# Norming the tokens of the last three experts apart, and finishing every other row while those experts still run

## The chip, the cores and the metric

The kernel runs on one core of a Trainium2 chip. The metric is the device time of one execution in microseconds (us). Before the change it is 1068.41 us, the median of 3 runs (1067.77 to 1070.65). TensorE is called PE, VectorE DVE, ScalarE ACT, GpSimd POOL, and SyncE SP. A DMA is issued by SP or, when its rows are picked by a list of indices, by POOL ("indirect").

## The reference

One layer of a hybrid decoder is computed for 1024 prompt tokens and 64 sample tokens of width 1024, all in float32: a mixing stage, cross-attention, and then the stage that matters here, a mixture of 32 experts in 4 groups, followed by the final norm.

```python
def hier_moe(x, w_rg, b_rg, w_re, b_re, w_e1, w_e3, w_e2):
    ...                                   # top-1 of 4 groups, top-2 of 8 experts within it
    for g in range(N_GROUPS):
        a = jnp.einsum('nd,edf->nef', xf, w_e1[g])
        b = jnp.einsum('nd,edf->nef', xf, w_e3[g])
        hid = jax.nn.silu(a) * b * gates[:, g, :, None]
        y = y + jnp.einsum('nef,efd->nd', hid, w_e2[g])
...
    x = x + hier_moe(rmsnorm(x, g_ffn), w_rg, b_rg, w_re, b_re, w_e1, w_e3, w_e2)
...
    y_prompt = rmsnorm(xp, g_final)       # x * rsqrt(mean(x*x) + 1e-6) * g_final, row by row
    y_sample = rmsnorm(xs, g_final)
```

A token gets rows from exactly two experts, both of one group.

## The kernel before, in words

Everything up to the routing fills the first 713 us. Then the loop over the experts runs (`e` from 0 to 31). Experts are taken in turn from the four groups (`expert_at`), so the last three (`e` = 29, 30, 31) belong to three different groups, and a token's other expert always lies a multiple of four steps away. An expert works on up to 128 listed tokens. Its steps are:

- POOL gathers the normed rows of its tokens from DRAM (`rows_in`, helper line 2466).
- PE turns them, and multiplies them with the "up" weights (`ab`); ACT applies SiLU (`sil`, line 1542), DVE multiplies the halves (`hid`, line 2314), PE turns the result (`hidden`, line 918), and ACT and DVE split it into a high and a low part (`hidden_left`, line 1206, and `hidden_lo`, line 2303).
- PE multiplies with the "down" weights one expert later (`yy(e - 1)`, matmuls in lines 525 to 527). Each product is made of three matmuls, because values are split into high and low parts; ACT (`part_to_hi`, line 1525) and DVE (`up_lo`, `down_lo`, lines 2292 and 2298) split every weight chunk of 128 x 1024.
- ACT scales the two halves of the result, 128 x 512 each, by the gates (`y_left`, line 1548), and POOL adds the rows to a DRAM tensor `token_sums` with an indirect DMA that accumulates (`rows_out`, line 2471). `token_sums` held x before the loop.

All engines run their own instruction streams in program order and meet by semaphores: `m_sc[0]` and `m_sc[1]` count landed scatters of even and odd experts, `m_w[s]` the weight loads, `m_used` the weight chunks that PE is done with, `m_yo0` and `m_yo1` the drained halves of the result. A weight chunk lies in one of 28 slots of a ring (`part_raw`).

After the loop, POOL waits until all 32 scatters have landed, and then lets the others go (`o_go`). A block for tokens that didn't fit into 128 slots ("spill") is skipped here. SP then loads the nine tiles of `token_sums` (8 of 128 prompt rows, one of 64 sample rows; line 989), ACT squares and sums each tile (line 1611) and takes roots for groups of tiles (`NORMS`, line 1614), DVE makes inverse roots in five small instructions (lines 2382 and 1632 to 1635) and scales each tile (line 2386), and SP stores it (line 1199).

Of the kernel before, what the change touches and what calls it, by code (L numbers as in the profile page):

```python
# [33 lines left out]
ALU = mybir.AluOpType  # L34
# [24 lines left out]
LG = 40  # L59
NEG = -3.0e38  # L60
# [22 lines left out]
def trunk_step(nc, i_, o_):  # L83
    ctx = ExitStack()
    with ctx:
# [210 lines left out]
        junk = regS[:, 4 * D:5 * D]  # L296
        gfin = regA[:, 7168:8192]
        NORMS = [(0, 2), (2, 3), (5, 3), (8, 1)]
# [68 lines left out]
        s_cst, s_pv, s_xh = sem("s_cst"), sem("s_pv"), sem("s_xh")  # L367
# [88 lines left out]
        s_moe = sem("s_moe")  # L456
# [18 lines left out]
        def sums_back(eng, t):  # L475

            eng.wait_ge(m_w[t], 16 * (len(range(t, 3 * NE, RAW // 2)) + 1))
# [12 lines left out]
        def _(pe):  # L490
# [435 lines left out]
            def yy(e):  # L926

                s = e % 2
                pe.wait_ge(m_hl, e + 1)
                if e >= 1:  # L930
                    pe.wait_ge(m_yo0, e)
                    pe.wait_ge(m_yo1, e)
                for c in range(2):
                    n = part_no["down", e, c]
                    hi, lo = part_hi[n % HI], part_lo[n % RAW]
                    pe.wait_ge(m_dl, 2 * e + c + 1)
                    for h in range(2):
                        product(bank[B_Y[h]][:, :], (HThi[s][:, c, :], HTlo[s][:, c, :]),
                                (hi[:, 512 * h:512 * h + 512], lo[:, 512 * h:512 * h + 512]),
                                c == 0, c == 1, m_used if h else None)  # L940
# [29 lines left out]
            pe.wait_ge(o_go, 1)  # L970
            n_spill = pe.value_load(spx[0:1, 16:17], min_val=0, max_val=SPILL)
            with pe.If(n_spill > 0):
                with pe.Fori(0, SPILL) as q:
# [13 lines left out]
        def _(sp):  # L987
# [23 lines left out]
            load(Y_f[:, 0:4, cols_of(0)], i_["xt"][:, 0:4, cols_of(0)], s_xh)  # L1011
# [168 lines left out]
            n_spill = sp.value_load(spx[0:1, 16:17], min_val=0, max_val=SPILL)  # L1180
            with sp.If(n_spill > 0):
                with sp.Fori(0, SPILL) as q:
# [9 lines left out]
            sp.wait_ge(s_moe, 1)  # L1192
            for t in range(NT):
                load(X[0:rows_of(t), t], sum_dram[P * t:P * t + rows_of(t), :], m_w[t])
            for t in range(NT):
                sp.wait_ge(s_fo, t + 1)
                dst = o_["y_prompt"][0, P * t:P * t + P, :] if t < NPT else \
                    o_["y_sample"].rearrange("b s d -> (b s) d")
                sp.dma_start(dst, X[0:rows_of(t), t]).then_inc(s_fst, 16)
            sp.wait_ge(s_fst, 16 * NT)  # L1200
# [3 lines left out]
        def _(act):  # L1204
# [45 lines left out]
            for h, landed in ((0, s_xh), (1, s_x[0])):  # L1250
# [315 lines left out]
            for e in range(2):  # L1566
                act.wait_ge(m_tx, e + 1)
                for q in range(2):
                    token_hi(e, q)
                if e == 0:  # L1570
                    part_to_hi("down", 0, 0)
                    part_to_hi("down", 0, 1)
            for e in range(NE):
                used(act, ("up", e, 3))
                sil(e % 2, B_AB[e % 2], m_sil)
                if e + 2 < NE:
                    part_to_hi("up", e + 2, 0)
                    act.wait_ge(m_tx, e + 3)
                    token_hi(e + 2, 0)
                    token_hi(e + 2, 1)  # L1580
                    part_to_hi("up", e + 2, 1)
                if e >= 1:
                    y_left(e - 1)
                if e + 2 < NE:
                    part_to_hi("up", e + 2, 2)
                hidden_left(e)
                if e + 2 < NE:
                    part_to_hi("up", e + 2, 3)
                if e + 1 < NE:
                    part_to_hi("down", e + 1, 0)  # L1590
                    part_to_hi("down", e + 1, 1)
            y_left(NE - 1)
            act.wait_ge(o_go, 1)
            n_spill = act.value_load(spx[0:1, 16:17], min_val=0, max_val=SPILL)
            with act.If(n_spill > 0):
                with act.Fori(0, SPILL) as q:
# [7 lines left out]
            nc.scalar.activation(small[:, 2:3], small[:, 0:1], ACT.Sqrt)  # L1604
            for t0, n in NORMS:
                for t in range(t0, t0 + n):
                    r = rows_of(t)
                    sums_back(act, t)
                    if t > 0:
                        act.wait_ge(s_fsq, t)  # L1610
                    nc.scalar.activation(junk[0:r, :], X[0:r, t, :], ACT.Square,  # L1611
                                         accum_out=stat[0:r, t:t + 1]).then_inc(s_fsq, 1)
                act.wait_ge(s_fsq, t0 + n)
                nc.scalar.activation(stat[0:r, 10 + t0:10 + t0 + n], stat[0:r, t0:t0 + n], ACT.Sqrt,  # L1614
                                     scale=1.0 / D, bias=small[0:r, 0:1]).then_inc(s_frt, 1)
# [3 lines left out]
        def _(dve):  # L1619
# [715 lines left out]
            down_lo(0, 1)  # L2335
            for e in range(NE):
                dve.wait_ge(m_sil, e + 1)
                hid(e % 2, B_AB[e % 2], m_hid)
                if e + 2 < NE:
# [3 lines left out]
                    up_lo(e + 2, 1)  # L2343
                hidden_lo(e)
# [3 lines left out]
                if e + 1 < NE:  # L2348
                    down_lo(e + 1, 0)
                    down_lo(e + 1, 1)  # L2350
                if e in (5, 8, 11):
                    place_in_table((e - 5) // 3)
                if e == 16:
                    spill_counts()
# [10 lines left out]
            dve.wait_ge(o_go, 1)  # L2365
            n_spill = dve.value_load(spx[0:1, 16:17], min_val=0, max_val=SPILL)
            with dve.If(n_spill > 0):
                with dve.Fori(0, SPILL) as q:
# [6 lines left out]


            def finish(g):
                t0, n = NORMS[g]
                r = rows_of(t0)
                dve.wait_ge(s_frt, g + 1)  # L2380
                a, root, r0, tmp, out = (stat[0:r, c + t0:c + t0 + n] for c in (280, 10, 300, 310, 20))
                link(ts_(a, stat[0:r, t0:t0 + n], 1.0 / D, EPS, ALU.mult, ALU.add))  # L2382
                inv_root(a, root, r0, tmp, out)
                for j in range(n):
                    x = X[0:r, t0 + j, :]
                    stt(x, x, out[:, j:j + 1], gfin[0:r, :], ALU.mult, ALU.mult).then_inc(s_fo, 1)  # L2386

            dve.wait_ge(s_cst, 32)
            for g in range(len(NORMS)):
                finish(g)  # L2390
# [3 lines left out]
        def _(g):  # L2394
# [5 lines left out]
            g.memset(bst[:, :], 1.0)  # L2400
            g.memset(lgm[:, :], 0.0)
# [42 lines left out]
            g.sem_inc(o_y, 1)  # L2444
# [10 lines left out]
            last_token, last_gate = g.to_reg(N - 1), g.to_reg(2 * P * NT - 1)  # L2455
            g.wait_ge(s_xnd[0], 16 * 5)
# [34 lines left out]

            rows_in(0)
# [6 lines left out]
            for e in range(NE):  # L2499
                if e + 4 < NE:  # L2500
                    rows_in(e + 4)
                if e >= 1:
# [11 lines left out]
            g.sem_inc(o_go, 1)  # L2514
# [12 lines left out]
            g.sem_inc(s_moe, 1)  # L2527
# [100 lines left out]
```

## Time and profile before

| | |
|---|---|
| median of 3 runs | 1068.41 us |
| the profiled execution | 1065.81 us |
| its span, first to last instruction | 1064.0 us |
| PE busy | 999.0 us (94%), 5327 matmuls |
| DVE busy | 638.3 us (60%) |
| ACT busy | 541.6 us (51%) |
| POOL busy | 197.6 us (19%) |
| last matmul starts | 1031.31 us |
| last store is issued | 1060.74 us |

The span is what the trace covers; the 1.8 us between it and the execution's own time are outside of it. A row of the timeline gives start, duration, engine, line, operation and what is written from what; in brackets stands how long the engine had been idle and what released it. Adjacent instructions of an engine overlap a little, so a series of the same kind is shorter than the sum of its durations.

### The profile page before, as it was taken

How to read it: one execution, taken by the hardware profiler on the slowest of the kernel's cores; microseconds unless marked ns; L12 is line 12 of the kernel's file. 1: busy time of each engine (PE TensorE's matmuls, PEld its weight loads, DVE VectorE, ACT ScalarE, POOL GpSimd, SP SyncE). 2: the span in 40 equal slices, each digit the busy share in tenths (PEclk: the TensorE clock that was granted, in tenths of full speed). 3: DMA queues.
4: the chain of work that ended last, by engine and by line, in shares of the span. 5: the costliest groups of instructions: out<-in, count | busy, mean ns of one | idle time of the engine just before them, and what ended most of it. 6: DMA issues, size and time to landing. Idle time of an engine off the chain costs nothing. (4 is left out here: it accounts for less than half of the span.)

```text
span 1064.0 us, 14237 instructions
## 1 busy us (share of the span) xinstructions
PE 999.0 (94%) x5327; PEld 848.1 (80%) x5327; DVE 638.3 (60%) x1175; ACT 541.6 (51%) x918; POOL 197.6 (19%) x136
## 2 busy tenths in 40 slices
PE   8999999999999999999999999948999999999970
PEld 6998999798887689999655878847888888888850
DVE  4526756345654650002664125677999999999935
ACT  6644333305221532213545012255999999999944
POOL 0003211100000021200000300011333375642220
PEclk9999999999999999999999999967999999999995
DMA  9701111244000653103563005487999999999738
GB/s 314 217 1 59 57 42 40 99 139 173 1 1 0 225 177 113 40 20 127 232 256 139 1 37 201 159 310 300 396 392 391 384 364 390 382 387 393 284 55 335
DMA packets 55211, 203.06 MB, mean 191 GB/s; under 512 B 10710, under 2 KB 19423, under 8 KB 41575
## 3 DMA queue, kind: packets, MB, share of 16 engines
q1 hardware_dynamic: 44327, 181.61, 44.9%
q0 software_dynamic: 10816, 20.54, 7.6%
q8 instruction: 43, 0.70, 0.3%
q14 instruction: 25, 0.20, 0.1%
HBM read 185.06 MB, written 32.83 MB: 205 GB/s over the span
## 5 line engine op out<-in xcount | busy, mean ns | idle before, releaser
L527 PE MATMUL bank<-regA_r,regW_r 128*128 128x352 f32 (+1 forms) x456 | 148.8, 326 | 0.0
L526 PE MATMUL bank<-regA_r,regW_r 128*128 128x352 f32 (+1 forms) x456 | 148.7, 326 | 0.0
L359 POOL TENSOR_TENSOR regW_r<-regW,regW_r 128x1024 fp32r<-128x1024 f32 x19 | 47.1, 2477 | 348.7 <-ACT regW_r L346 348.6
L1525 ACT ACTIVATE regY_r<-expert_w 128x1024 fp32r<-128x1024 f32 x105 | 108.9, 1062 | 1.0 <-PE bank L527 0.9
L525 PE MATMUL bank<-expert_w_r,regS_r 128*128 128x512 f32 x256 | 103.4, 404 | 0.0
L1525 ACT ACTIVATE regW_r<-expert_w 128x1024 fp32r<-128x1024 f32 x87 | 90.2, 1061 | 6.7 <-PE bank L527 6.7
L2292 DVE TENSOR_TENSOR expert_w_r<-expert_w,regY_r 128x1024 fp32r<-128x1024 f32 x74 | 89.0, 1218 | 0.0
L525 PE MATMUL bank<-regY_r,regW_r 128*128 128x352 f32 (+1 forms) x264 | 87.3, 331 | 0.5 <-ACT regB L1206 0.5
L526 PEld LDWEIGHTS bank<-regA_r,regW_r 128*128 128x128 f32 x456 | 85.9, 188 | 0.4
L527 PEld LDWEIGHTS bank<-regA_r,regW_r 128*128 128x128 f32 x456 | 85.6, 188 | 0.0
L2466 POOL DMA_INDIRECT regW<-normed_tokens,idx x32 | 44.0, 1374 | 200.0 <-DVE idx L2201 119.6
L1215 ACT ACTIVATE regS<-regX 128x1024 f32<-128x1024 f32 (+1 forms) x17 | 18.0, 1060 | 119.9 <-DVE regX L1877 119.9
L527 PE MATMUL bank<-regW_r,regA_r 128*128 128x384 f32 (+3 forms) x216 | 76.4, 354 | 0.0
L2471 POOL DMA_INDIRECT token_sums<-regS,idx x32 | 55.5, 1735 | 106.2 <-ACT regS L1548 102.6
L1877 DVE TENSOR_TENSOR regX<-regX,bank 128x512 f32<-128x512 f32 (+1 forms) x36 | 24.1, 686 | 77.8 <-PE bank L527 77.7
L527 PE MATMUL bank<-regY_r,regS_r 128*128 128x512 f32 x180 | 70.4, 391 | 0.0
L526 PE MATMUL bank<-regY_r,regB_r 128*128 128x512 f32 (+1 forms) x176 | 68.6, 390 | 0.0
L1952 DVE TENSOR_REDUCE stat<-bank 128x2 f32<-128x512 f32 x16 | 11.0, 690 | 93.9 <-PE bank L699 93.9
L2292 DVE TENSOR_TENSOR expert_w_r<-expert_w,regW_r 128x1024 fp32r<-128x1024 f32 x54 | 64.8, 1217 | 0.0
L527 PE MATMUL bank<-regY_r,regA_r 128*128 128x512 f32 (+1 forms) x164 | 64.0, 390 | 0.0
L525 PE MATMUL bank<-regB_r,regW_r 128*128 128x352 f32 (+1 forms) x192 | 63.0, 328 | 0.0
L526 PE MATMUL bank<-regY_r,regS_r 128*128 128x512 f32 x148 | 57.7, 390 | 0.0
(363 smaller groups left out, 2408.1 us busy)
## 6 DMA issues: line engine op xcount, KB each, us to landing
expert_w<-in_we SPq DMA_DIRECT2D x96, 1024.0 KB, 13.3
regY<-in_cache_mem_v SPq DMA_DIRECT2D x6, 1024.0 KB, 7.2
regW<-in_wbc SPq DMA_DIRECT2D x11, 512.0 KB, 3.6
regS<-in_x_prompt SPq DMA_DIRECT2D x8, 512.0 KB, 6.5
regX<-in_x_prompt SPq DMA_DIRECT2D x8, 512.0 KB, 6.6
regW<-in_wq SPq DMA_DIRECT2D x8, 512.0 KB, 3.6
regA<-in_kct SPq DMA_DIRECT2D x4, 1024.0 KB, 7.9
token_sums<-regX SPq DMA_DIRECT2D x8, 512.0 KB, 2.9
```

The costliest lines, as they stand in the source:

```text
L359: eng.tensor_tensor(lo, raw, hi.bitcast(F32), ALU.subtract).then_inc(w_lo[name], 1)
L525: nc.tensor.matmul(out, stays[0], moves[1], start=first, stop=False)
L526: nc.tensor.matmul(out, stays[1], moves[0], start=False, stop=False)
L527: ins = nc.tensor.matmul(out, stays[0], moves[0], start=False, stop=last)
L1215: nc.scalar.activation(dst[0:r, :], src[0:r], ACT.Square, accum_out=stat[0:r, c:c + 1]).then_inc(s_sq[s], 1)
L1525: nc.scalar.activation(part_hi[u % HI], part_raw[n % RAW], ACT.Copy).then_inc(m_wh, 1)
L1877: tt(x, x, ps[0:r, :], ALU.add).then_inc(sg, 1)
L1952: link(nc.vector.tensor_reduce(stat[:, 276:278], ps[:, :].rearrange("p (a m) -> p a m", a=2), axis=AX.X, op=ALU.max, negate=True))
L2292: tt(part_lo[n % RAW], part_raw[n % RAW], part_hi[u % HI].bitcast(F32), ALU.subtract).then_inc(m_ul, 1)
L2466: g.indirect_dma_start(out=XG[s], out_offset=None, in_=xn_dram, in_offset=bass.IndirectOffsetOnAxis(ap=ix[:, 0:1], axis=0), bounds_check=l ...
L2471: g.indirect_dma_start(out=sum_dram, out_offset=bass.IndirectOffsetOnAxis(ap=ix[:, 0:1], axis=0), in_=YO[s], in_offset=None, bounds_check= ...
```

## The change

The tokens of the last three experts (`LATE = 3`) are kept out of `token_sums`. Their sums so far are gathered into SBUF early, DVE adds the last expert rows to them there, and these three blocks of 128 rows are normed and written by indirect DMAs straight to the outputs. The nine tiles are loaded as soon as the scatters of experts 0 to 28 have landed, are normed, and are stored as before; the rows in them that belong to late tokens are stale and are overwritten afterwards. Dead slots of the weight ring hold all of it (`spot`).

- POOL: at `e` = 28, after `rows_out(27)`, `late_sums()` gathers three times; `rows_out` of 29, 30 and 31 are gone. At the end, `samples_out(0)`, `samples_out(1)`, a wait for all prompt stores (`s_fst`), `prompt_out(0)` to `(2)`, `samples_out(2)`: six indirect DMAs. The wait for all of them stands ahead of the spill block.
- SP: loads of `gfin` and the nine tiles move ahead of the end of the loop; stores follow in the order of `UNITS` (sample tile, prompt tiles 0 to 7).
- ACT: `y_left` of 29, 30 and 31 is gone. Three squares stand at the end of `e` = 30, ahead of `sil(31)`. Behind `sil(31)` come the table load for Sqrt, the first root and a fourth square, ahead of `hidden_left(31)`. Eight more squares and three roots follow the loop.
- DVE: `rows_left(29)`, `(30)`, `(31)` add `bank * gate` to the gathered rows. Units 0 and 1 are multiplied by `gfin` ahead of time (`weighted`), so that a plain scaling is left. Four groups of inverse roots (`ROOTS`) and twelve scaled blocks instead of nine. Two small index operations come at `e` = 14 (`late_samples`).
- PE: the first half of the last expert's result is signalled by itself. The spill block is taken only if there is a spill, on every engine.

```diff
@@ names
+LATE = 3
-        NORMS = [(0, 2), (2, 3), (5, 3), (8, 1)]
+        LAST = len(PARTS) - RAW
+        def spot(j):
+            return part_raw[(LAST + j) % RAW]
+        UNITS = [("tile", t) for t in (NPT, *range(NPT))] + [("rows", k) for k in range(LATE)]
+        ROOTS = [(0, 3), (3, 4), (7, 1 + LATE), (NT + LATE - 1, 1)]
+        AHEAD, WEIGHTED = (3, 2) if LATE > 2 else (0, 0)
@@ sync
-            used(sp, ("down", NE - 1, 1))
+            for n in range(NT):
+                weights_landed(sp, n)
+            spot_dead(sp, GFIN_AT)
             load(gfin, i_["gfin"], s_cst)
-            sp.wait_ge(o_go, 1)
+            for q in range(2):
+                sp.wait_ge(m_sc[q], 16 * len(range(q, NE - LATE, 2)))
...
+            for u, (_, t) in enumerate(UNITS[:NT]):
+                spot_dead(sp, XF_AT + u)
+                sums_load(t)
+            for u, (_, t) in enumerate(UNITS[:NT]):
+                sp.wait_ge(s_fo, u + 1)
+                final_store(t)
@@ scalar, in the loop over e
+                if e == NE - 1:
+                    nc.scalar.activation(small[:, 2:3], small[:, 0:1], ACT.Sqrt)
+                    if AHEAD:
+                        roots(*ROOTS[0])
+                        square(AHEAD)
-                if e >= 1:
+                if 1 <= e <= NE - LATE:
                     y_left(e - 1)
...
+                if e == NE - 2:
+                    part_to_hi("down", e + 1, 1)
+                    for u in range(AHEAD):
+                        square(u)
+            for u, n in ROOTS[1 if AHEAD else 0:]:
+                for v in range(max(u, AHEAD + 1 if AHEAD else 0), u + n):
+                    square(v)
+                roots(u, n)
@@ vector
+            def rows_left(e):
+                k = e - (NE - LATE)
+                rows_back(dve, k)
+                gates = gate_of_slot[:, expert_at(e):expert_at(e) + 1]
+                for h, signal in ((0, m_yo0), (1, m_yo1)):
+                    if e == NE - 1 and h == 0:
+                        dve.wait_ge(full[B_Y[0]], uses[B_Y[0]] + 1)
+                    else:
+                        used(dve, ("down", e, 1))
+                    rows = XR[k][:, 512 * h:512 * h + 512]
+                    stt(rows, bank[B_Y[h]][:, :], gates, rows, ALU.mult, ALU.add).then_inc(signal, 1)
...
+                if e == NE - 1 and AHEAD:
+                    weighted(1)
+                if e > NE - LATE:
+                    rows_left(e - 1)
                 hidden_lo(e)
...
+            for k, (u, n) in enumerate(ROOTS):
+                dve.wait_ge(s_frt, k + 1)
+                inverse(u, n)
+                for v in range(u, u + n):
+                    scaled(v)
+                if k == 0 and AHEAD:
+                    rows_left(NE - 1)
@@ gpsimd
+            def late_sums():
+                for q in range(2):
+                    g.wait_ge(m_g[q], 16 * (NE // 2))
+                for k in range(LATE):
+                    e = NE - LATE + k
+                    g.wait_ge(m_sc[e % 2], 16 * len(range(e % 2, e - NG + 1, 2)))
+                    if k >= 2:
+                        rows_back(g, k - 2)
+                    spot_dead(g, XR_AT + k)
...
-            rows_out(NE - 1)
-            for s in range(2):
-                g.wait_ge(m_sc[s], 16 * (NE // 2))
...
+            g.wait_ge(s_xh_ys, 32)
+            for k in range(LATE - 1):
+                samples_out(k)
+            g.wait_ge(s_fst, 16 * NPT)
+            for k in range(LATE):
+                prompt_out(k)
+            samples_out(LATE - 1)
+            for q in range(2):
+                g.wait_ge(m_sc[q], 16 * scattered[q])
```

## Rows read from the trace of the kernel before

**Rows 1.** Chain that ended last, in time: start, us, what

```profile
1033.82 1.55 DMA token_sums<-regS,idx
1035.37 2.50 issue
...
1040.73 7.05 DMA regX<-token_sums
```

**Rows 2.** Timeline of PE, experts 30 and 31

```profile
1026.43 0.38 PE L918 MATMUL bank<-cst,regW 128*128 128x128 f32 x2
1028.68 0.50 PE L525 MATMUL bank<-expert_w_r,regW_r 128*128 128x512 f32 x1 [1.87 <-DVE regW_r L2303]
...
1031.31 0.39 PE L527 MATMUL bank<-regW_r 128*128 128x512 f32 x1
```

**Rows 3.** Timeline of ACT and DVE, experts 30 and 31

```profile
1018.20 1.27 ACT L1548 ACTIVATE regS<-bank,rv 128x512 f32<-128x512 f32 x2 [2.34 <-PE bank L527]
...
1020.72 2.36 DVE L2298 TENSOR_TENSOR expert_w_r<-expert_w,regW_r 128x1024 fp32r<-128x1024 f32 x2 [0.52 <-ACT regW_r L1525]
...
1023.91 0.38 ACT L1542 ACTIVATE regY<-bank 128x256 f32<-128x256 f32 x1 [2.27 <-PE bank L527]
...
1026.63 1.27 ACT L1548 ACTIVATE regS<-bank,rv 128x512 f32<-128x512 f32 x2 [2.34 <-PE bank L527]
1027.79 0.38 ACT L1206 ACTIVATE regW_r<-bank 128x256 fp32r<-128x256 f32 x1
1028.20 0.42 DVE L2303 TENSOR_TENSOR regW_r<-bank,regW_r 128x256 fp32r<-128x256 f32 x1 [3.46 <-ACT regW_r L1206]
```

**Rows 4.** Timeline of the last 26 us, SP, ACT and DVE

```profile
1038.93 4.76 SPq L989 DMA_DIRECT2D regX<-token_sums  x9
1040.05 0.20 ACT L1604 ACTIVATE small<-small 128x1 f32<-128x1 f32 x1
1042.63 1.06 ACT L1611 ACTIVATE regS<-regX 128x1024 f32<-128x1024 f32 x1 [2.38 <-DMA regX<-token_sums]
...
1043.88 1.06 ACT L1611 ACTIVATE regS<-regX 128x1024 f32<-128x1024 f32 x1
...
1049.32 0.17 DVE L2382 TENSOR_SCALAR stat<-stat 128x3 f32<-128x3 f32 x1 [0.37 <-ACT stat L1614]
...
1050.33 3.68 DVE L2386 SCALAR_TENSOR_TENSOR regX<-regX,stat,regA 128x1024 f32<-128x1024 f32 x3
```

**Rows 5.** Timeline of ACT where it turns from Exp to Sqrt

```profile
632.20 0.18 ACT L1215 ACTIVATION_READ_ACCUMULATOR regS<-regX 128x1 f32 x1
632.40 1.28 ACT L1218 ACT_TABLE_LOAD   x1
633.70 0.29 ACT L1218 ACTIVATE stat<-stat,small 128x1 f32<-128x1 f32 x1
```

**Rows 6.** Groups of DVE instructions by shape: busy us, mean ns

```profile
L2310 DVE TENSOR_TENSOR regS_r<-bank,regS_r 128x512 fp32r<-128x512 f32 x64 | 41.0, 683 | 1.7 <-ACT regS_r L1529 1.7
L1651 DVE TENSOR_SCALAR regS<-regX,stat 128x1024 f32<-128x1024 f32 x8 | 6.0, 754 | 0.3
```

**Rows 7.** POOL's indirect DMAs, one view by line: ns min/median/max

```profile
L2471 POOL DMA_INDIRECT token_sums<-regS,idx x32: 1552/1606/2315, 748.5 to 1033.8; - x32
L2466 POOL DMA_INDIRECT regW<-normed_tokens,idx x32: 992/1390/2123, 713.2 to 988.6; - x32
L2450 POOL DMA_INDIRECT place_table<-pay,plc x18: 961/1936/2093, 853.9 to 930.3; - x18
```

**Rows 8.** Timeline of POOL

```profile
715.14 1.03 POOL L2466 DMA_INDIRECT regW<-normed_tokens,idx  x1 [0.30 <-issue]
...
1002.49 1.77 POOL L2471 DMA_INDIRECT token_sums<-regS,idx  x1 [6.88 <-ACT regS L1548]
1011.81 1.55 POOL L2471 DMA_INDIRECT token_sums<-regS,idx  x1 [7.55 <-ACT regS L1548]
...
1028.64 1.55 POOL L2471 DMA_INDIRECT token_sums<-regS,idx  x1 [6.75 <-ACT regS L1548]
```

**Rows 9.** Stores of line 1199, view of the line

```profile
DMA to landing us min/median/max: 2.9/5.0/6.5
```

More of the change, by code:

```diff
@@ L473, in kv_used, with weights_landed, sums_back, late_at @@
                 eng.wait_ge(s_kvd, c)
-        def sums_back(eng, t):
-            eng.wait_ge(m_w[t], 16 * (len(range(t, 3 * NE, RAW // 2)) + 1))
+        def weights_landed(eng, s):
+            eng.wait_ge(m_w[s], 16 * len(range(s, 3 * NE, RAW // 2)))
+        def sums_back(eng, n, again=0):
+            eng.wait_ge(m_w[n], 16 * (len(range(n, 3 * NE, RAW // 2)) + 1 + again))
+        def late_at(k):
+            return (NE - LATE + k) % 2
+        def rows_back(eng, k):
+            eng.wait_ge(m_g[late_at(k)], 16 * (NE // 2 + k // 2 + 1))
+        def spot_dead(eng, j):
+            used(eng, PARTS[LAST + j])
         def used(eng, part):
@@ L1009, in u_load @@
                 load(regB[:, c:c + 2 * DA], i_["wu"][:, c:c + 2 * DA], s_wu_kc[q])
[L1011 removed]
+            load(Y_f[:, 0:4, cols_of(0)], i_["xt"][:, 0:4, cols_of(0)], s_xh_ys)
             load(pv[:, :], i_["pv"], s_pv)
@@ L1190, in _ @@
                                  .rearrange("a p k -> (a p) k")).then_inc(o_ix, 16)
[L1192 to L1200, printed above, removed]
+                sp.wait_ge(o_go, 2)
+                for t in range(NT):
+                    sums_load(t)
+                for t in range(NT):
+                    sp.wait_ge(s_fo, NT + t + 1)
+                    final_store(t)
+                sp.wait_ge(s_fst, 16 * 2 * NPT)
+                sp.wait_ge(s_xh_ys, 48)
         @block.scalar
@@ L1249, in _ @@
             nc.scalar.activation(small[:, 1:2], small[:, 0:1], ACT.Sqrt)
-            for h, landed in ((0, s_xh), (1, s_x[0])):
+            for h, landed in ((0, s_xh_ys), (1, s_x[0])):
                 act.wait_ge(landed, 16)
@@ L1572, in _, with square, roots @@
                     part_to_hi("down", 0, 1)
+            def square(u):
+                kind, n = UNITS[u]
+                r = rows_of(n) if kind == "tile" else P
+                if kind == "tile":
+                    sums_back(act, n)
+                else:
+                    act.wait_ge(m_yo0, NE - LATE + n + 1)
+                    act.wait_ge(m_yo1, NE - LATE + n + 1)
+                if u > 0:
+                    act.wait_ge(s_fsq, u)
+                nc.scalar.activation(junk[0:r, :], (XF if kind == "tile" else XR)[n][0:r, :], ACT.Square,
+                                     accum_out=stat[0:r, u:u + 1]).then_inc(s_fsq, 1)
+            def roots(u, n):
+                act.wait_ge(s_fsq, u + n)
+                nc.scalar.activation(stat[:, 20 + u:20 + u + n], stat[:, u:u + n], ACT.Sqrt,
+                                     scale=1.0 / D, bias=small[:, 0:1]).then_inc(s_frt, 1)
             for e in range(NE):
@@ L1588, in _ @@
                     part_to_hi("up", e + 2, 3)
-                if e + 1 < NE:
+                if e + 1 < NE and e != NE - 2:
                     part_to_hi("down", e + 1, 0)
                     part_to_hi("down", e + 1, 1)
-            y_left(NE - 1)
-            act.wait_ge(o_go, 1)
+                if e == NE - 2:
+                    part_to_hi("down", e + 1, 1)
[5 more added lines that the diff above has]
+                roots(u, n)
             n_spill = act.value_load(spx[0:1, 16:17], min_val=0, max_val=SPILL)
             with act.If(n_spill > 0):
+                act.wait_ge(o_go, 1)
+                nc.scalar.activation(small[:, 2:3], small[:, 0:1], ACT.Silu)
                 with act.Fori(0, SPILL) as q:
@@ L1603, in _ @@
                     y_half(0, 0, gate_spilled, o_yo)
-            nc.scalar.activation(small[:, 2:3], small[:, 0:1], ACT.Sqrt)
-            for t0, n in NORMS:
-                for t in range(t0, t0 + n):
+                nc.scalar.activation(small[:, 2:3], small[:, 0:1], ACT.Sqrt)
+                for t in range(NT):
                     r = rows_of(t)
[L1608 to L1611, printed above, removed]
+                    sums_back(act, t, 1)
+                    act.wait_ge(s_fsq, NT + LATE + t)
+                    nc.scalar.activation(junk[0:r, :], XF[t][0:r, :], ACT.Square,
                                          accum_out=stat[0:r, t:t + 1]).then_inc(s_fsq, 1)
-                act.wait_ge(s_fsq, t0 + n)
-                nc.scalar.activation(stat[0:r, 10 + t0:10 + t0 + n], stat[0:r, t0:t0 + n], ACT.Sqrt,
-                                     scale=1.0 / D, bias=small[0:r, 0:1]).then_inc(s_frt, 1)
+                    act.wait_ge(s_fsq, NT + LATE + t + 1)
+                    nc.scalar.activation(stat[0:r, 20 + t:21 + t], stat[0:r, t:t + 1], ACT.Sqrt,
+                                         scale=1.0 / D, bias=small[0:r, 0:1]).then_inc(s_frt, 1)
         @block.vector
@@ L2335, in _, with late_samples, inverse, scaled @@
             down_lo(0, 1)
+            def late_samples():
+                listed_at, samples_at = idx[:, expert_at(NE - LATE):NE:EPG], idx[:, NE:NE + LATE]
+                link(ts_(samples_at, listed_at, float(SEQ), float(NOWHERE), ALU.is_lt, ALU.mult))
+                link(stt(samples_at, samples_at, -float(SEQ), listed_at, ALU.add, ALU.add))
+            def inverse(u, n, r=P):
+                a, root, r0, tmp, out = (stat[0:r, c + u:c + u + n] for c in (40, 20, 60, 80, 100))
+                link(ts_(a, stat[0:r, u:u + n], 1.0 / D, EPS, ALU.mult, ALU.add))
+                inv_root(a, root, r0, tmp, out)
+            def scaled(u):
+                kind, n = UNITS[u]
+                g = stat[:, 100 + u:101 + u]
+                if u < WEIGHTED:
+                    x = XF[n][0:rows_of(n), :]
+                    ts_(x, x, g[0:rows_of(n), :], None, ALU.mult).then_inc(s_fo, 1)
+                elif kind == "tile":
+                    x = XF[n][0:rows_of(n), :]
+                    stt(x, x, g[0:rows_of(n), :], gfin[0:rows_of(n), :], ALU.mult, ALU.mult).then_inc(s_fo, 1)
+                else:
+                    spot_dead(dve, YR_AT + n)
+                    stt(YR[n], XR[n], g, gfin, ALU.mult, ALU.mult).then_inc(s_rows, 1)
+            def weighted(u):
+                t = UNITS[u][1]
+                x = XF[t][0:rows_of(t), :]
+                dve.wait_ge(s_fsq, u + 1)
+                link(tt(x, x, gfin[0:rows_of(t), :], ALU.mult))
+            def rows_left(e):
[5 more added lines that the diff above has]
+                        dve.wait_ge(full[B_Y[0]], uses[B_Y[0]] + 1)
+                    else:
+                        used(dve, ("down", e, 1))
+                    rows = XR[k][:, 512 * h:512 * h + 512]
+                    stt(rows, bank[B_Y[h]][:, :], gates, rows, ALU.mult, ALU.add).then_inc(signal, 1)
             for e in range(NE):
@@ L2374, in _ @@
                     y1(0, o_yo)
[L2377 to L2390, printed above, removed]
+                for t in range(NT):
+                    r = rows_of(t)
+                    dve.wait_ge(s_frt, len(ROOTS) + t + 1)
+                    inverse(t, 1, r)
+                    x = XF[t][0:r, :]
+                    stt(x, x, stat[0:r, 100 + t:101 + t], gfin[0:r, :], ALU.mult, ALU.mult).then_inc(s_fo, 1)
         @block.gpsimd
```

73 lines of the change are left out of this document (62 added, 11 removed).

## The prediction

> **What bounds the kernel now.** I read the chain of waits first, then the timeline of the last 50 us. The change touches nothing ahead of expert 28 except two tiny operations, so only the end counts. The last matmul starts at 1031.31 [rows 2] and the span ends at 1064.0: 32.3 us of tail in which PE does nothing. The chain shows what the tail is made of. The last scatter takes 1.55 us to issue and 2.50 us to land [rows 1]; the nine loads start at 1038.93 [rows 4] and the fifth is back at 1047.78 [rows 1]; from 1049.32 on DVE works almost without a gap, 1.0 us of small operations and then 3.68 us for three tiles, each group again [rows 4]; the last store is issued at 1060.74 and the span ends 3.3 us later. So the tail is a wait for the last scatter, a reload of data that was mostly final long before, and the norm of 1088 rows.
>
> **How the new end goes, part by part.** Times are on the clock of the profiled execution.
>
> *Early gathers (POOL).* The scatter of expert 27 is issued at 1002.49 and the next at 1011.81 [rows 8]. Between them go three gathers at 0.99 to 1.6 us [rows 7], the third behind the landing of the first: 1004.3 + 2 x 1.9 for two, landing 2.5 us after its issue (the row of the scatter, [rows 1]), so the third goes out near 1009.4 and ends near 1011.0. It fits; nothing is queued behind it but the scatter of expert 28, which waits for ACT anyway. Cost 0, up to 0.5 us if gathers take the 2.1 us maximum.
>
> *Loads of the sums (SP).* They wait for the scatter of expert 28: 1011.81 + 1.55 + 2.50 = 1015.9. The first 512 KB load takes 1042.63 - 1038.93 = 3.7 us, and later tiles follow at 1.3 us each (from 1042.63 to 1047.78 for four) [rows 1, 4]. The sample tile (half the size) is back at about 1019.1, tile 0 at 1020.4, tile 1 at 1021.7, tile 2 at 1023.0 and the last at 1029.5. The weights are all there by then, so these loads have the DMA engines alone.
>
> *ACT at expert 30.* The scaling of expert 29's result goes (1.27 us at 1018.20 [rows 3]). A weight split moves ahead of `hidden_left(30)`, whose input comes at 1018.4, and hides there. Three squares of 1.25 us (1042.63 to 1043.88 [rows 4]) follow from 1019.8: they end at 1023.5, just ahead of the 1023.91 at which `sil(31)` starts [rows 3]. Cost 0 with 0.4 us to spare; a further 1.7 us of delay would hide under PE's `yy(30)`: its end released ACT at 1026.63 [rows 3], and `th(31)` stands behind it [rows 2].
>
> *ACT at expert 31.* `sil(31)` ends at 1024.3. Then the table load of 1.28 us, a dummy of 0.2, a root of 0.3, a square of 1.25: 1027.3. `hidden_left(31)` starts there instead of at 1027.79, since the 1.27 us of `y_left(30)` at 1026.63 are gone [rows 3]. What the table load costs I take from [rows 5]: 1.30 us from its start to the next instruction, and 0.02 us between the instruction before it and the load. The Trainium skill (ScalarE: Activation LUTs, "What ACT_TABLE_LOAD costs") adds about 1.38 us of drain to each load, 2.66 us in all. By that rule `hidden_left(31)` would start at 1028.7 and everything behind it about 0.8 us later; the trace doesn't show such a drain.
>
> *DVE up to the last matmuls.* `rows_left(30)` needs the end of `yy(30)` at 1026.6 and takes two halves of 0.68 us that overlap a little, 1.3 us (the row of a 128x512 operation from PSUM, [rows 6]): 1027.9. `hidden_lo(31)` follows, 1027.9 to 1028.35, against 1028.20 to 1028.62 before [rows 3]. So DVE now holds what ACT held, and the last matmuls start 0.3 us ahead of the 1028.68 of before [rows 2]. `hid(31)` isn't moved: `rows_left(29)` runs from 1018.2 to 1019.5, `hidden_lo(30)` to 1019.9, the two `down_lo(31)` (2.36 us) to 1022.2 instead of 1020.72 to 1023.08, the early product with `gfin` (1.2 us) to 1023.5, and `sil(31)` ends at 1024.3 [rows 3].
>
> *DVE to the end.* From 1028.35 DVE has no reason to stop:
> - inverse roots of group 1: 1.0 (1049.32 to 1050.33 [rows 4]); two plain scalings at 0.67 (0.75 less the overlap, [rows 6]) and one full one at 1.28: 1032.0
> - `rows_left(31)`: 1.3: 1033.3. Its operands are there at 1030.8 and 1031.5.
> - group 2: 1.0 + 4 blocks at 1.20 and 0.08 more (3.68 us for three, [rows 4]), 4.9: 1039.2
> - group 3: 1.0 + 4.9: 1045.1. Tiles 6 and 7 are ready at 1041.5 and 1042.7, the first two late blocks at 1043.9 and 1045.1.
> - group 4: 1.0 + 1.3: 1047.4.
>
> ACT isn't the bound: from 1027.7 its squares at 1.25 and roots at 0.3 give the groups' roots at 1031.7, 1037.1 and 1038.7, all ahead of DVE (1033.3, 1039.2, 1045.1).
>
> *POOL to the end.* Six indirect DMAs follow one another. The first waits for the block at 1043.9 and starts 0.74 us after it (ACT done at 1026.63 + 1.27 = 1027.90, POOL at 1028.64 [rows 3, 8]). No row shows a plain indirect write of 4 KB rows to DRAM. Its nearest rows [rows 7] bound it: 0.99 us (shortest gather) to 1.94 us (median of the table writes). I take 1.55, that of the scatters of the same rows with nothing beside them [rows 8]. Between two lie 0.30 us [rows 8]. So 1043.9 + 0.74 + 6 x 1.55 + 5 x 0.30 = 1055.4. The fence on prompt stores hides: tile 7's store goes out at 1042.8 and takes 2.9 us at least, 5.0 as the median [rows 9], so it is passed at 1045.7 to 1047.8, and POOL reaches it at 1048.0. The last block at 1047.4 hides too. The last DMA lands 2.5 us after its issue [rows 1] and POOL needs about 0.35 us for its last waits: 1058.3.
>
> **The sum.** 1064.0 - 1058.3 = 5.7 us less. The profiled execution, 1065.8 us, becomes 1060.1; it lay 2.6 us under the median, so the median becomes 1068.4 - 5.7 = 1062.7. Of the 32.3 us behind the last matmul 27 stay: what the loads and the wait for the scatter took is now filled by DVE's series (to 1047.4) and POOL's (1043.9 to 1058.3). With the issue at 0.99 us six of them save 3.4 us more (1059.3); with 1.94 they cost 2.3 more (1065.1). The two index operations at expert 14 cost some 0.4 us of DVE in a loop where DVE has such gaps: 0.
>
> **Rivals.**
> - *POOL is quick, and DVE is the bound.* With 0.99 us for each issue the time is 1059.3. For it: the second of two gathers in a row took 1.03 us [rows 8]. Against it: no scatter took under 1.55 [rows 7]. Chance 0.14.
> - *The squares need their own table.* Square in front of `sil(31)` runs where SiLU's table is in place. In this trace Square ran with Exp's table and no load, since the load came only with the root behind it [rows 5]; with SiLU's no row shows it. The Trainium skill (ScalarE: Activation LUTs, "Table sets: the hidden batching unit") names relu, copy, identity and abs as being in every set, not Square. If it is missing, a load stands ahead of the squares and another ahead of `sil(31)`, 1.3 us each; `sil(31)` ends at 1026.9, and `hidden_left(31)` starts 2.6 us later, at 1029.9. DVE's series and the end slip by 2.0 us or a little more: 1064.9. Chance 0.07.
> - *The fence decides.* If tile 7's store takes the longest of its kind, 6.5 us [rows 9], the fence is passed at 1049.3 and the four DMAs behind it start 0.74 us later, at 1050.0 instead of 1048.3: 1064.4. For it: the stores follow each other at DVE's 1.2 us, near the 1.3 us that a tile takes on the DMA engines. Against: the loads are over by then. Chance 0.09.
> - *Slower: the indirect DMAs queue.* The trace has long rows twice in a row (two gathers), not six times. If the writer of the queue has to wait until earlier ones have landed before it has room, the last four each pay the landing of 2.5 us: +10 us, 1072.7, slower by 4.3. It decides from 1.4 us for each of the four on (5.7 / 4). Against it: only 0.30 us of idle time lie ahead of the second of two gathers [rows 8]. Chance 0.06.
> - *The gain is eaten at the experts.* ACT works in order, so late sums hold up `sil(31)` and PE. Tile 1 would have to be back 2.6 us later than 1021.7 to move PE, and some 8 us later to cost the whole gain. A load that takes the 7.1 us of a tile in the queue [rows 1] isn't enough. 1067 to 1069. Chance 0.04.
>
> **How the numbers follow.** The forecast has 0.60: 1062.7, from 1060.5 to 1065.1 by itself. The range to 8 in 10 takes in the quick POOL, the fence and the tables: 1059.0 to 1066.0. A measurement here can tell 0.3%, 3.2 us. Over 3.2 us faster: nearly all of the forecast (0.56), the quick POOL (0.14), most of the fence (0.07) and of the tables (0.05): 0.82. Within: the rest of these and late sums, 0.11. Slower: queueing and the worst of late sums, 0.07.
>
> **What would show it.** Right: the last matmul starts at 1031.0; DVE has one block from 1028 to 1047 with under 1 us of gaps; ACT shows one table load, behind `sil(31)`; the six DMAs of POOL start at 1044.6 and stand 1.85 us apart; the chain ends in POOL. Wrong: idle time of POOL that is released by a store (fence); a PE gap over 1.9 us at expert 31 (ACT late); two more table loads; gaps of over 1 us between POOL's DMAs. The forecast is worth least in the length of a plain indirect write, which counts six times.

## The result, and the profile after

The changed kernel takes 1072.55 us (median of 20 runs), against 1068.66 us for the kernel before, measured beside it. The ratio is 1.0032, with a 95% interval of 1.0024 to 1.0040: 3.4 us slower (0.32% of 1068.7; the medians are 3.9 us apart, the means 3.4). One execution of e2 below (2058 us, in a slower state) is left out of its ratio. The forecast was 5.7 us faster, and its range ended at 1066.0.

| | before | after |
|---|---|---|
| the profiled execution | 1065.81 us | 1072.67 us |
| its span | 1064.0 us | 1070.5 us |
| last matmul starts | 1031.31 us | 1039.88 us |
| last DVE instruction ends | 1060.7 us | 1054.8 us |
| POOL's last indirect DMA is issued, done at | 1035.4 us | 1060.8 us |

Part of this is drift ahead of the change: the scatter of expert 27, the last instruction that both kernels share in the same place, starts at 1002.49 in one [rows 8] and at 1004.32 in the other. From here on I count from that start ("t"). So counted, the span ends at t = 61.5 before and t = 66.2 after.

The chain that ended last, of the changed kernel (start, us, what), its first part and its end:

```profile
1006.36 2.08 DMA expert_w<-token_sums,idx
1008.44 0.30 issue
1008.75 1.93 POOL expert_w L2641
1010.67 5.03 issue
...
1015.91 0.47 POOL expert_w L2641
...
1017.99 6.39 DMA token_sums<-regS,idx
...
1024.40 3.48 DMA expert_w<-token_sums
...
1027.90 1.16 ACT regY L1633 x2
...
1030.38 1.15 ACT regY L1633 x2
...
1032.24 1.23 DVE expert_w L2449
...
1035.32 0.79 PE bank L554
...
1059.84 0.98 POOL out_y_sample L2669
```

In the kernel before the chain began with the last scatter, after all matmuls [rows 1]. Here it begins at expert 28, with a gather that was meant to cost nothing, and goes from there through a scatter, the load of the first tile and ACT's squares to the last experts.

POOL in the timeline of the changed kernel (line 2609 scatters, 2641 gathers the late sums):

```profile
1004.32 1.74 POOL L2609 DMA_INDIRECT token_sums<-regS,idx  x1 [6.91 <-PE bank L556]
1006.36 2.08 POOL L2641 DMA_INDIRECT expert_w<-token_sums,idx  x1 [0.30 <-issue]
1008.75 1.93 POOL L2641 DMA_INDIRECT expert_w<-token_sums,idx  x1 [0.30 <-issue]
1015.91 1.78 POOL L2641 DMA_INDIRECT expert_w<-token_sums,idx  x1 [5.24 <-issue]
1017.99 2.58 POOL L2609 DMA_INDIRECT token_sums<-regS,idx  x1 [0.30 <-issue]
1052.27 1.28 POOL L2669 DMA_INDIRECT out_y_sample<-expert_w,idx  x1 [31.70 <-DVE expert_w L2442]
1053.85 1.83 POOL L2669 DMA_INDIRECT out_y_sample<-expert_w,idx  x1 [0.30 <-issue]
1055.99 0.98 POOL L2669 DMA_INDIRECT out_y_prompt<-expert_w,idx  x1 [0.30 <-issue]
...
1059.84 0.98 POOL L2669 DMA_INDIRECT out_y_sample<-expert_w,idx  x1 [0.30 <-issue]
```

POOL is idle for 5.24 us ahead of the third gather, and the scatter of expert 28 starts only behind it, 13.67 us after that of expert 27 instead of 9.32 [rows 8]. The six stores at the end are cheap: 0.98 us from the third on.

What the late scatter does further on is in the list of waits (engine, line, waited for: us in total, times, longest):

```profile
ACT regY L1633 <- DMA expert_w<-token_sums: 6.3, 1, 6.3
DVE expert_w L2449 <- ACT regY L1633: 5.0, 1, 5.0
PE bank L947 <- DVE regW L2396: 4.0, 1, 4.0
PE bank L554 <- DVE regW_r L2385: 2.5, 1, 2.5
```

and in two stretches (busy us of PE, PEld, DVE, ACT, POOL; granted clock; DMA share; GB/s):

```profile
1028.00:1032.40 4.40, 0.43 (x3) 0.02 (x1) 1.72 (x3) 4.20 (x8) 0.00 (x0) 1.00 1.03 410
1035.30:1039.50 4.20, 4.18 (x10) 3.31 (x11) 3.31 (x8) 3.98 (x8) 0.00 (x0) 0.50 0.86 261
```

ACT stood before its squares with nothing to do until 1027.90, and `sil(31)` is behind them in its stream. PE did almost nothing for 4 us, waited 2.5 us more for DVE, and then ran nine of its last twelve matmuls with half the clock granted (0.50, that is 1.2 instead of 2.4 GHz): 0.43 us from one to the next, against 0.23 before [rows 2].

The second surprise stands behind POOL's last store. Its issue ends at 1060.8 and the span at 1070.5. The view of the line at which all engines leave the program has what lies between (duration in ns, start in us):

```profile
L86 POOLq DRAIN  x1: 7747/7747/7747, 1062.5 to 1062.5; - x1
```

The kernel before has the same instruction, started at 1039.2 and so over long before the end:

```profile
L85 POOLq DRAIN  x1: 7502/7502/7502, 1039.2 to 1039.2; - x1
```

### The profile page after: what moved, and what is told of

The parts are those of the page before. It is cut to its first block and busy times, and to the rows that moved or that the text cites. A ratio compares the mean times of both kernels' runs of the same rounds, so it can differ in the third digit from the quotient of the medians.

```text
span 1070.5 us, 14272 instructions
## 1 busy us (share of the span) xinstructions
PE 1000.0 (93%) x5327; PEld 848.9 (79%) x5327; DVE 647.8 (61%) x1188; ACT 540.8 (51%) x918; POOL 208.8 (20%) x143
## 5 line engine op out<-in xcount | busy, mean ns | idle before, releaser
L2609 POOL DMA_INDIRECT token_sums<-regS,idx x29 | 51.9, 1790 | 79.5 <-ACT regS L1597 72.3
```

Of the source, the lines that this page charges most:

```text
L2609: g.indirect_dma_start(out=sum_dram, out_offset=bass.IndirectOffsetOnAxis(ap=ix[:, 0:1], axis=0), in_=YO[s], in_offset=None, bounds_check= ...
```

## The experiments

Two theories stood after this. *Order*: the indirect DMAs land late at this point of the kernel, the third gather waits for that, the scatter of expert 28 behind it, and SP, ACT and PE behind the scatter. *Drain*: POOL needs 7.5 to 7.75 us at the program's end, whatever it did last, and the change made POOL the last engine. Each had a rival.

### e1: the third gather behind the scatter of expert 28

```diff
                 if e == NE - 4:
-                    late_sums()
+                    late_sums(range(2))
+                if e == NE - 3:
+                    late_sums(range(2, LATE))
```

> The changed kernel, with the third gather of the late sums moved behind the scatter of expert 28 on POOL. Theory (order): in the changed kernel POOL was held before the third gather until 1015.7 us, because the first gather had landed only then, and the scatter of expert 28 stood behind it (issued 13.7 us after that of expert 27 instead of 9.3); the tiles of the sums came 4 to 5 us late from that, ACT's squares held up expert 31, and PE ended at half clock. So here the scatter of expert 28 goes out about 9.3 us after that of expert 27, PE has no gap over 2.5 us at expert 31, and the time falls by 5 to 6 us against the changed kernel, to 1 to 2.5 us under the kernel before. Rival (landing): the scatter and the tiles themselves take so long to land that ACT is late in any order; then the gain is 2 us at most and PE's gap of 4 us stays.

Measured: 1067.35 us, ratio to the kernel before 0.9993 (0.9981 to 1.0005). Against the changed kernel (1.0032) that is 0.39%, 4.2 us less, over twice what the rival allowed. The order theory holds; its size was a miss, since it had asked for 5 to 6 us. The timeline of POOL in e1:

```profile
1002.61 1.72 POOL L2609 DMA_INDIRECT token_sums<-regS,idx  x1 [6.92 <-PE bank L556]
...
1012.07 1.60 POOL L2609 DMA_INDIRECT token_sums<-regS,idx  x1 [3.09 <-ACT regS L1597]
1013.97 2.04 POOL L2641 DMA_INDIRECT expert_w<-token_sums,idx  x1 [0.30 <-issue]
```

The scatter goes out 9.46 us after its forerunner. The timelines of SP, ACT and PE in e1 tell why a little was left over:

```profile
1017.33 4.89 SPq L1018 DMA_DIRECT2D expert_w<-token_sums  x9
...
1024.47 1.06 ACT L1633 ACTIVATE regY<-expert_w 128x1024 f32<-128x1024 f32 x1 [1.18 <-DMA expert_w<-token_sums]
...
1029.41 0.50 PE L554 MATMUL bank<-expert_w_r,regW_r 128*128 128x512 f32 x1 [2.48 <-DVE regW_r L2385]
```

From the scatter's start to the first load of a tile pass 5.26 us, not the 4.06 that I had added up from the last scatter [rows 1]. The third square, of tile 1, starts 7.1 us after that load, where the forecast had the tile back after 5.8. ACT still waits for tiles (2.2 us in two waits), PE's gap is 2.48 us instead of 1.87 [rows 2], and the clock falls here too (0.61 granted from 1030.0 to 1033.5).

### e2: the last wait moved from POOL to SP

```diff
@@ gpsimd
-            for q in range(2):
-                g.wait_ge(m_sc[q], 16 * scattered[q])
             with g.If(n_spill > 0):
+                for q in range(2):
+                    g.wait_ge(m_sc[q], 16 * scattered[q])
@@ sync
             sp.wait_ge(s_xh_ys, 32)
+            for q in range(2):
+                sp.wait_ge(m_sc[q], 16 * scattered[q])
```

> The changed kernel, with the last wait for the six indirect stores moved from POOL to SP. Theory (drain of fixed length): POOL's instruction at the program's end, a drain of 7.75 us, starts right behind the last issue instead of 1.5 us later, and has its length whatever is in flight; the time falls by 1.3 to 1.6 us against the changed kernel. Rival (the drain waits for what is in flight): it starts earlier but ends at the same time, difference under 0.5 us.

Measured: 1069.81 us, ratio 1.0015 (1.0000 to 1.0030), 0.17% or 1.8 us less than the changed kernel. The intervals overlap, so the time alone doesn't show a fixed length, and in e2's profile the scatter of expert 28 also happened to come 2.4 us earlier; the trace of e2 is clearer, again in the view of the exit line:

```profile
L86 POOLq DRAIN  x1: 12504/12504/12504, 1053.9 to 1053.9; - x1
```

POOL's sequencer is through with the program at 1053.9, while four DMAs are still being issued. The drain then ends at 1066.4, which is 7.8 us behind the end of the last issue (1057.64 + 0.98). In the changed kernel the drain ends 9.4 us behind it (1060.8 to 1070.3), since the last wait stands between them. Its length is the same 7.75 us there, so it counts from POOL's last work or last wait, whichever is later.

### e3: the kernel before, with POOL as the last engine

```diff
             g.wait_ge(s_kout, 32)
+            g.wait_ge(s_fst, 16 * NT)
```

> The kernel before, with one wait more: POOL waits for the nine output stores before it ends, as SP does. Theory (a drain of fixed length, hidden in the kernel before because POOL is done at 1039 us): POOL's drain of 7.5 us starts at 1063.7 and the time rises by 7.5 us. Rival (the drain covers only indirect DMAs issued shortly before it): 25 us after the last of them there is nothing left to cover, and the time rises by under 0.5 us.

Measured: 1076.8 us, ratio 1.0074 (1.0058 to 1.0090): 7.9 us slower (four runs) from one wait that never holds up any work. The drain theory holds, and the rival is out: POOL had issued its last indirect DMA 28 us earlier. The view of the exit line in e3:

```profile
L85 POOLq DRAIN  x1: 7502/7502/7502, 1068.8 to 1068.8; - x1
```

### e4: both edits

> The changed kernel with both edits: third gather behind the scatter of expert 28, last wait on SP. If the order and the drain are separate costs they add up: 6.5 to 7.5 us less than the changed kernel, 2.5 to 3.5 us less than the kernel before. If the landing rival or the in-flight rival holds, 2 us or less of it is left, and the kernel stays slower than before.

Measured: 1066.91 us, ratio 0.9983 (0.9972 to 0.9993). This version is a little faster than both kernels: 1.8 us under the kernel before, 5.2 us (0.49%) under the changed one. The gains of e1 and e2 add up to 6.0 us; I had expected 6.5 to 7.5, and 2.5 to 3.5 us under the kernel before, so this too came out smaller. PE's timeline in e4:

```profile
1033.22 0.50 PE L555 MATMUL bank<-expert_w_r,regW_r 128*128 128x512 f32 x1 [2.06 <-DVE regW_r L2388]
```

The gap ahead of the last matmuls is nearly that of before, and the full clock stays to the end of PE's work (0.39 us for each of the last matmuls).

### e5: nothing ahead of the end of the experts

```diff
-        AHEAD, WEIGHTED = (3, 2) if LATE > 2 else (0, 0)
+        AHEAD, WEIGHTED = (0, 0)
```

> The changed kernel, with AHEAD and WEIGHTED at 0: ACT does no square and DVE no product for the final norm before the end of the experts. Theory (PE's stall comes from ACT's squares, and the tail is a series of DVE): PE has no gap over 2.5 us at expert 31 and ends 6 us earlier, but DVE then has all twelve blocks behind it at 1.22 us and four groups of inverse roots at 1.0, which ends about 1 us earlier than in the changed kernel: time 0.5 to 2 us less than the changed kernel, 2 to 3.5 us more than the kernel before. Rival (the stall of PE is the whole loss): 5 us or more less than the changed kernel.

Measured: 1071.44 us, ratio 1.0026 (1.0011 to 1.0041): no clear difference from the changed kernel, and not the 5 us of the rival. PE has one gap, of 1.68 us, and its last matmul starts at t = 28.6 instead of 35.6, yet DVE ends at t = 48.2 instead of 50.5.

The fair partner for this profile is e2's. There the work ahead, with three squares before `sil(31)`, is in place, and the tiles' loads start at t = 16.6, almost as here (16.4). PE's timeline in e2:

```profile
1030.65 0.44 PE L948 MATMUL bank<-cst,regW 128*128 128x128 f32 x2 [2.28 <-DVE regW L2399]
1033.59 0.79 PE L555 MATMUL bank<-expert_w_r,regW_r 128*128 128x512 f32 x1 [2.50 <-DVE regW_r L2388]
```

With equally late tiles the work ahead costs PE 4.8 us (last matmul at t = 33.4 against 28.6), and DVE ends at t = 48.3 against 48.2. Freeing PE by this edit returns nothing at DVE's end: what PE gains, DVE has to do later.

### e6: four experts apart

```diff
-LATE = 3
+LATE = 4
```

> The changed kernel with LATE = 4: expert 28 is kept apart too, so no scatter stands behind the gathers, and the tiles wait for the scatter of expert 27 (landed near 1013). Theory: PE's stall goes (6 us), but DVE gets one block more (1.2 us) and POOL two indirect stores more at 1.3 us each: 2 to 3.5 us less than the changed kernel, within 2 us of the kernel before. Rival (landing): the tiles are late whatever they wait for, and with more work behind it the time rises above that of the changed kernel.

Measured: 1070.79 us, ratio 1.0035 (1.0018 to 1.0051). Expected were 2 to 3.5 us less than the changed kernel, measured is no less: a miss. The stall of ACT is gone, but another one has come; DVE's timeline in e6:

```profile
1012.78 1.41 DVE L2462 SCALAR_TENSOR_TENSOR expert_w<-bank,rv,expert_w 128x512 f32<-128x512 f32 x2 [1.94 <-DMA expert_w<-token_sums,idx]
```

DVE adds the rows of expert 28 to the first gathered block one expert earlier than in the changed kernel, and that block, gathered from 1003.65, isn't there until 1012.7. PE waits 1.9 us for DVE at expert 30, and the last matmul starts at t = 31.1, 2.3 us later than before. It is the same late landing, met by another engine. How much of the miss it explains is not shown: e6's profiled execution (1068.87) is its fastest, and the stores of POOL take 11.0 us instead of 8.5.

### e7: a semaphore of its own for the third gather

```diff
+        m_g2 = sem("m_g2")
...
-                    if k >= 2:
-                        rows_back(g, k - 2)
...
-                                         bounds_check=last_token, oob_is_err=False).then_inc(m_g[late_at(k)], 16)
+                                         bounds_check=last_token, oob_is_err=False).then_inc(m_g2 if k == 2 else m_g[late_at(k)], 16)
```

(What reads the third block waits for `m_g2` in place of `m_g[late_at(k)]`.)

> The changed kernel, with a semaphore of its own for the third gather, so that it no longer waits for the landing of the first gather, but still for that of expert 27's scatter, which it reads. In the changed kernel the scatter had landed at 1013.3 and the gather at 1015.7. If both waits are as the trace shows, the third gather and with it the scatter of expert 28 go out about 2 us earlier, and the time falls by 1.5 to 2.5 us against the changed kernel. Rival (the scatter's landing alone holds POOL): no change, under 0.7 us.

Measured: 1069.53 us, ratio 1.0010 (0.9995 to 1.0024), 0.22% or 2.3 us less than the changed kernel, within what was expected; the two intervals just touch. POOL's timeline in e7:

```profile
1014.06 1.99 POOL L2643 DMA_INDIRECT expert_w<-token_sums,idx  x1 [1.77 <-DMA token_sums<-regS,idx]
```

The third gather is now released by the scatter of expert 27, which it must read behind. It goes out at t = 8.1, earlier than in any run with both waits (9.3 at the earliest), so both waits held it. Against e1 some 2 us are left, about half. That share is weakly shown: the tiles' loads start at t = 16.5 here, no earlier than in e2 (16.6) and e5 (16.4), which keep both waits.

### e8: the kernel before, with the three gathers added

```diff
+            def late_sums():                       # into dead slots, read by nobody
+                for q in range(2):
+                    g.wait_ge(m_g[q], 16 * (NE // 2))
+                for k in range(3):
+                    e = NE - 3 + k
+                    g.wait_ge(m_sc[e % 2], 16 * len(range(e % 2, e - NG + 1, 2)))
+                    if k >= 2:
+                        g.wait_ge(m_g[1], 16 * (NE // 2 + 1))
...
+                if e == NE - 4:
+                    late_sums()
             rows_out(NE - 1)
```

> The kernel before, with the three gathers of the changed kernel added at expert 28, in the same place and with the same waits, into dead slots that nobody reads, and a wait for them at POOL's end. Nothing else of the change. Theory: the third gather holds POOL until all indirect DMAs of the last weights' time have landed (7 us behind their issue), and the scatter of expert 28 goes out 13 us after that of expert 27, as in the changed kernel, but nobody waits for it before 1026, so the time stays within 1 us of the kernel before. Rival (the gathers disturb weights or scatters by their traffic): PE stalls at experts 29 to 31 and the time rises by 2 us or more.

Measured: 1067.53 us, ratio 0.9999 (0.9987 to 1.0010). So the gathers' own traffic costs nothing that could be measured, and the rival is out. The scatter of expert 28 came 10.6 us after that of expert 27 here, not the 13 that I had written: POOL was held for 1.3 us and not for 4, and this cost nothing either. That a longer hold would be free too was not tested.

### All runs on one scale

Times of the timelines, in us from the start of expert 27's scatter:

| | scatter 28 | tiles' loads | last matmul | DVE's end | POOL's last issue, end | span's end |
|---|---|---|---|---|---|---|
| before | 9.3 | 36.4 | 28.8 | 58.2 | 32.9 | 61.5 |
| forecast | 9.3 | 13.4 | 28.5 | 44.9 | 53.0 | 55.8 |
| changed | 13.7 | 20.1 | 35.6 | 50.5 | 56.5 | 66.2 |
| e1 | 9.5 | 14.7 | 30.6 | 45.7 | 51.7 | 61.4 |
| e2 | 11.3 | 16.6 | 33.4 | 48.3 | 54.3 | 62.3 |
| e3 | 9.3 | 36.2 | 28.8 | 57.9 | 32.9 | 68.8 |
| e4 | 9.5 | 14.7 | 29.0 | 44.9 | 50.9 | 58.9 |
| e5 | 11.1 | 16.4 | 28.6 | 48.2 | 54.2 | 63.9 |
| e6 | none | 8.8 | 31.1 | 48.2 | 55.4 | 65.3 |
| e7 | 10.4 | 16.5 | 30.1 | 46.0 | 52.0 | 61.7 |
| e8 | 10.6 | 36.5 | 28.8 | 58.2 | 32.9 | 61.5 |

e2 and e5 have the POOL order of the changed kernel, and their scatter of expert 28 came at 11.3 and 11.1, not 13.7. So how long the third gather is held differs from one execution to the next by 2 us or more; with one profile of each kernel, what is typical stays open. The profiled execution of the changed kernel (1072.67) lies at its median. The last column, taken against the kernel before, follows the measured times within 1.3 us (changed kernel: 4.7 against 3.4 us; e4: -2.6 against -1.8; e3: 7.3 against 7.9).

The profiles also show what goes with the long holds. In the 4 us from t = 0 on, the queue of SP's loads (the last weights and `gfin`) fills 61% of the DMA engines in the changed kernel and in e6, and the first gathered block is there at t = 11.4 and 11.2. In e2, e5 and e8 it fills 42, 38 and 29%, and the third gather, which waits for that block, goes out at t = 10.0, 9.8 and 9.3. This is an order among five profiles, not an experiment.

## Why the prediction was wrong

**What bounded the kernel before** was read rightly: a tail of 32.3 us behind the last matmul, of which the reload could go.

**Early gathers: this step failed.** The forecast gave a gather 2.5 us from the end of its issue to its landing, a value taken from the last scatter [rows 1], when nothing else is on the DMA engines. In the stretch of the gathers the last weights still arrive (see above). In the changed kernel the third gather, which waits for the first, goes out at 1015.91, 7.5 us behind the end of the first one's issue (1008.44); e6 shows a block that isn't there 7 us after its issue ended (1005.7 to 1012.7), and e7 that the scatter of expert 27 takes nearly as long (it holds POOL until 1014.06, 6.4 us behind the end of its issue). The gathers don't make it so: in the kernel before, which has none, packets of this scatter still move 6.6 us after its issue has ended (until t = 8.4). So the trace of before had a nearer row than the one that I took. That it is the weights' traffic which delays them fits the profiles, but no run took the traffic away. The forecast had the third gather at 1009.4, and "nothing is queued behind it but the scatter of expert 28, which waits for ACT anyway". It was exactly that scatter that everything else hung on. I had named the queue and priced it at up to 0.5 us; it came to 4.4 us in the profiled execution, and 4.2 us of time by e1.

**Loads of the sums.** Forecast at t = 13.4, found at 20.1: 4.4 from the order, and the rest because the scatter took 6.39 us from its start to its landing, not 4.06. In e1 5.26 us passed to the first load.

**ACT at experts 30 and 31.** The mechanism stood as the last rival, with a chance of 0.04: squares in ACT's stream ahead of `sil(31)`, so that late tiles become a stall of PE. The trace shows it step by step. It was priced too low in three ways. First, the slack of 2.6 us was too large. Its 1.7 us "under PE's `yy(30)`" hold for PE's turning of `hid(31)` alone, but the table load, the root and the fourth square also stand between `sil(31)` and `hidden_left(31)`, and delay goes through them undiminished. From the start of the third square (tile 1) to the last group of matmuls pass 4.94 us in the changed kernel (1030.38 to 1035.32) and in e1 (1024.47 to 1029.41) alike. In the kernel before that group starts at t = 26.2 [rows 2], so the slack behind the forecast 1021.7 was 2.0 us. In e1 tile 1 came 2.6 us late, and PE was moved. Second, the clock: after the gaps nine of PE's last matmuls ran at 0.50, 0.43 us apart instead of 0.23, which is 1.8 us. Third, the loads of the tiles began 6.7 us later than forecast. The table load behaved as [rows 5] had it: one load, 1.29 us from its start to the next instruction, with the squares ahead of it in SiLU's table. The drain of 1.38 us that the Trainium skill (ScalarE: Activation LUTs, "What ACT_TABLE_LOAD costs") adds isn't in this trace, and the rival with a table of its own for Square is out.

**DVE to the end.** 15.2 us from the start of `rows_left(31)` to the last block, forecast 15.4 (1032.0 to 1047.4). Right.

**POOL to the end.** The issue was mis-sized on the high side: six at 1.55 were expected, found were 1.28, 1.83 and four of 0.98, with 0.30 between. From the start of the first to the end of the last 8.5 us instead of 10.8. The landing took 1.2 us, not 2.5. The rival with a quick POOL was nearer. The fence, the wait for all prompt stores, didn't hold POOL (0.30 us ahead of the first prompt store), and nothing queued. The rival with queueing DMAs had named 1072.7 us, and 1072.55 were measured: that is chance, since its mechanism isn't in the trace.

**The end of the program: the step that was missing.** The forecast gave 0.35 us to "its last waits". Behind them stands the drain of 7.75 us. It was in the trace of the kernel before, but hidden under the final norm, and neither the chain nor the timeline lists it; the view of the exit line does. e3 prices it alone at 7.9 us.

Put together on the scale of t: 55.8 forecast, + 7.1 for the last matmul (35.6 instead of 28.5), - 1.5 for DVE's end behind it (14.9 us instead of 16.4), - 2.0 for POOL (8.05 us behind DVE's end forecast, 6.0 found), + 6.8 for what follows the last issue (9.7 instead of 2.85) = 66.2, the span's end. By this sum the change would have won without the drain in spite of the stall (59.4 against 61.5); no run tests that. Without the late scatter (e1) it breaks even.

## What to carry to other kernels

Before work is moved to an engine's end, look at what that engine does at the exit of the program, and which engine leaves last: here POOL's leave costs 7.5 to 7.9 us, is free while another engine works longer than that, and a single wait is enough to expose it. Price a DMA's landing from rows of the same stretch, with the same traffic, not from the quiet tail. And when an instruction stream gets a new wait, follow the one instruction queued behind it to everyone who will wait for it *in the new kernel*: in the old one the first to wait for that scatter was ACT's scaling of expert 30's result, 14.8 us after its issue [rows 3, 8]; in the new one SP's loads waited for its landing, and ACT for them.

## What the runs showed of the hardware

- POOL's drain lasts 7.50 us in the kernel before, with one wait more (e3) or without, 28 us after the last indirect DMA as well as 4 us after it. It lasts 7.71 us in e8, 7.75 in the changed kernel and 7.91 in e6, and ends 7.8 us behind the last issue where the sequencer had arrived there early (e2). POOL issues 82 indirect DMAs in the kernel before, 85 in e8, 88 in the changed kernel and 90 in e6, the same order; what sets the length is open.
- Indirect stores of 4 KB rows to DRAM, without accumulation, take POOL 0.98 us each in a series; scatters that accumulate took 1.55 at least [rows 7].
- After gaps of PE of 4.0 and 2.5 us the granted clock was halved for the matmuls behind them (changed kernel), also behind gaps of 2.28 and 2.50 us (e2), and behind the single gap of 2.48 us in e1, from the sixth matmul after it on. With gaps of 0.41 and 2.50 us (e7), of 2.06 us (e4) and of 1.87 us (before) it stayed full. So the length of the last gap alone doesn't tell these runs apart; what does is open.
